# Stick-breaking attention: the second scores of a step issued earlier in TensorE's queue, and one row copy moved up in ScalarE's

## The chip, the cores and the metric

The kernel runs on one core of a Trainium2 chip. The metric is the device time of one execution in microseconds (us); lower is better. Engines: TensorE (PE in the profile, its weight loads PEld), VectorE (DVE), ScalarE (ACT), GpSimd (POOL), and SyncE (SP), which issues most of the transfers.

## The reference, cut to what matters

Two decoder layers over 1024 tokens of width 1024, in float32. Layer 0 mixes tokens with a gated MLP, layer 1 with stick-breaking attention; after each mixer comes a squared-ReLU MLP of hidden width 4096. The change lies in the attention alone, which has 16 heads of 64 and query blocks of 128 rows:

```python
z = einsum('bthd,bshd->bhts', qb, kb) * scale
log_keep = where(causal, log_sigmoid(-z), 0.0)
survive  = cumsum(log_keep, axis=-1, reverse=True) - log_keep
a        = where(causal, exp(log_sigmoid(z) + survive), 0.0)
out      = einsum('bhts,bshd->bthd', a, vb)
```

So each weight is sigmoid(z) times the product of (1 - sigmoid(z)) over the later keys.

## The kernel before, in words

The attention runs as a loop over 8 pairs of heads (`att_step(i)`, i = 0 to 7). A head has 8 tiles, one for each block of 128 query rows; tile t has (t + 1) x 128 keys. Tiles are worked off in pairs (2m, 2m + 1). A step n of `att_step` finishes one pair, m = `ORDER[n % 4]`, with ORDER = 0, 1, 3, 2; there are 8 steps per i, four for each of the two heads. Four steps in a row (m = 0, 1, 3, 2) are called a round here, and its steps a, b, c and d. There are 16 rounds.

What happens to a tile, and the letters used from here on (the figure behind S, B, Q, R and M is the tile of its head, the figure behind K, A and V is the group g of two key blocks):

- S: `scores` on TensorE writes z into one of two PSUM buffers, that of the tile's parity (L1238), then adds the causal mask (L1240). It waits for the R of the tile before the last one, which frees the buffer.
- B: `break_tile` on ScalarE, the sigmoid of z, from PSUM to SBUF (L1654).
- Q: `keep_tile` on ScalarE, the sigmoid of -z, in place in PSUM (L1660).
- R: `sticks` on VectorE, the running product along the row (L2142). It waits for Q.
- M: `stick_mult` on GpSimd, B's result times the shifted product (L910).
- K: `to_keys` on TensorE, up to four transposes of 128x128 of the pair's weights, of key blocks 2g and 2g + 1 (L1255), into one of two PSUM banks in turn. It waits for the copy A that read that bank before.
- A: `keys_in` on ScalarE, which copies a K's bank to SBUF (L1668).
- V: `values` on TensorE, the products of A's result with v (L1268). They run one step later than the K and A of their group.

A pair m has groups g = 0 to m. In step n the scores are those of the pair two steps ahead, `scores(i, 2n + 4)` and `scores(i, 2n + 5)`: tiles 6 and 7 in step a, 4 and 5 in step b, 0 and 1 in step c (of the next head), 2 and 3 in step d. Each engine works its instructions off in the order in which they were written; between engines there are semaphores only. After every other step ScalarE and VectorE also evict a finished output (`out_hi`, L1675, and `out_lo`, L2149). In the first `att_step`, ScalarE and GpSimd also split two blocks of the next stage's weights (L1333, L804), behind steps n = 2 and n = 4.

The order of a round on TensorE before, with V of the step ahead:

```
step a: S6  K0 V0           S7  V1 V2
step b: S4  K0 V0 K1        S5
step c: S0  K0 V0 K1 K2     S1  K3 V1
step d: S2  K0 V0 K1 K2     S3  V1 V2 V3
```

and on ScalarE:

```
step a: B6 A0 Q6    B7 Q7
step b: B4 A0 Q4 A1 B5 Q5        out_hi
step c: B0 A0 Q0 A1 B1 Q1 A2 A3
step d: B2 A0 Q2 A1 B3 Q3 A2     out_hi
```

Of the kernel before, what the change touches and what calls it, by code (L numbers as in the profile page):

```python
# [175 lines left out]
def wait(eng, sem, value):  # L176

    if isinstance(value, int) and value <= 0:
        return
    eng.wait_ge(sem, value)  # L180
# [17 lines left out]
def iterate(eng, n, emit):  # L198

    emit(0)  # L200
    if n > 2:
        with eng.Fori(1, n - 1) as i:
            emit(i)
    if n > 1:
        emit(n - 1)
# [16 lines left out]
QP = NT // 2  # L222
# [4 lines left out]
def pair(n):  # L227

    return ORDER[n % QP]


def groups_before(n):

    return (n // QP) * GH + sum(m + 1 for m in ORDER[:n % QP])


def tile_of(k):

    m, e = pair(k // 2), k % 2
    return (k // NT) % 2, m, e, 2 * m + e  # L240


def build(nc, x, g_mix_pre, g_mix_post, g_ffn_pre, g_ffn_post, w_in, v_g, v_b, w_s, b_s, w_aout,
          w_qkv, w_bout, w1, w2, out):
    ctx = ExitStack()
    with ctx:
# [682 lines left out]
        def _(pe):  # L929
# [297 lines left out]
            def scores(i, k):  # L1227

                hb, _, zb, tb = tile_of(k)
                if tb == 0:  # L1230
                    pe.wait_ge(qk_in[hb], (i + k // (2 * NT)) * (6 * 16) + 6 * 16)
                wait(pe, stick_done, i * (2 * NT) + (k - 1))
                s = (tb + 1) * P
                for c0 in range(0, s, HALF):

                    c1 = c0 + max(2 * P, min(HALF, s - c0))
                    for n in range(2):
                        mm = pe.matmul(z_ps[zb][:, c0:c1], q_st[hb][:, tb * P:(tb + 1) * P], k_st[hb][n][:, c0:c1],  # L1238
                                       start=(n == 0), stop=(n == 1 and c1 < s))
                mm = pe.matmul(z_ps[zb][:, s - P:s], ident_bf[:], mask_bf[:], start=False, stop=True)  # L1240
                mm.then_inc(z_done, 1)

            def to_keys(i, n, g):

                m, gi = pair(n), groups_before(n) + g
                if g == 0:
                    pe.wait_ge(a_done, i * (2 * NT) + (2 * n + 2))
                wait(pe, aT_in, i * (2 * GH) + (gi - 1))
                for p in (2 * g, 2 * g + 1):
                    for e in range(2):  # L1250
                        if p == 0 and e == 0:
                            continue
                        col = (1 - e) * P + (2 * m + 1 - p) * P
                        at_col = (p % 2) * 2 * P + e * P
                        mm = pe.transpose(psum[:, 4 + gi % 2, at_col:at_col + P], brk[m][e][:, col:col + P], ident[:])  # L1255
                mm.then_inc(aT_psum, 1)

            def values(i, n, g):

                m, hb = pair(n), (n // QP) % 2  # L1260
                if g == 0 and n % QP == 0:
                    pe.wait_ge(vh_in[hb], i * 16 + 16)
                if g == 0 and n % 2 == 0:

                    wait(pe, o_split, i * 4 + (n // 2 - 1))
                pe.wait_ge(aT_in, i * (2 * GH) + (groups_before(n) + g + 1))
                for p in (2 * g, 2 * g + 1):
                    mm = pe.matmul(psum[:, 6 + m // 2, (m % 2) * 2 * P:(m % 2 + 1) * 2 * P],  # L1268
                                   v_st[hb][:, 2 * m + 1 - p, :], aT[n % 2][:, p * 2 * P:(p + 1) * 2 * P],
                                   start=(p == 0), stop=(p == 2 * m + 1))  # L1270
                mm.then_inc(av_done, 1)

            def att_step(i):
                first, last = isinstance(i, int) and i == 0, isinstance(i, int) and i == HEADS // 2 - 1
                if first:
                    for k in range(4):
                        scores(0, k)
                    pe.wait_ge(rows_set, 2)
                for n in range(2 * QP):
                    more = not (last and n >= 2 * QP - 2)  # L1280
                    if more:
                        scores(i, 2 * n + 4)

                    here = pair(n) + 1
                    before = 0 if first and n == 0 else pair(n - 1) + 1

                    def prior(g):
                        if g < before:
                            if n:
                                values(i, n - 1, g)  # L1290
                            else:
                                values(i - 1, 2 * QP - 1, g)

                    to_keys(i, n, 0)
                    prior(0)
                    for g in range(1, min(3, here)):
                        to_keys(i, n, g)
                    if more:
                        scores(i, 2 * n + 5)
                    if here > 3:  # L1300
                        to_keys(i, n, 3)
                    for g in range(1, 4):
                        prior(g)
            iterate(pe, HEADS // 2, att_step)
            for g in range(pair(2 * QP - 1) + 1):
                values(HEADS // 2 - 1, 2 * QP - 1, g)
# [4 lines left out]
            for u in range(D // UC):  # L1311
                ready(U_O + u)
                last = u == D // UC - 1
                for t in range(NT):

                    before = 3 if not last or t < 2 else 1
# [12 lines left out]
        def _(act):  # L1329
            def hi(n, b, w=wt, raw=stage):  # L1330

                act.wait_ge(unit_landed, n * 16 + 16)
                act.activation(w[b][0][:], raw[:], ACT.Copy).then_inc(unit_hi, 1)  # L1333
# [315 lines left out]
            def break_tile(i, k):  # L1649
                _, m, e, tb = tile_of(k)  # L1650
                act.wait_ge(z_done, i * (2 * NT) + (k + 1))

                wait(act, aT_psum, i * (2 * GH) + groups_before(k // 2 - QP + 1))
                act.activation(brk[m][e][:, (1 - e) * P:(2 * m + 2) * P], z_ps[e][:, 0:(tb + 1) * P],  # L1654
                               ACT.Sigmoid, scale=SCALE).then_inc(brk_done, 1)

            def keep_tile(i, k):
                _, m, e, tb = tile_of(k)
                act.wait_ge(brk_done, i * (2 * NT) + (k + 1))
                act.activation(z_ps[e][:, 0:(tb + 1) * P], z_ps[e][:, 0:(tb + 1) * P],  # L1660
                               ACT.Sigmoid, scale=-SCALE).then_inc(keep_done, 1)

            def keys_in(i, n, g):
                gi, c0 = groups_before(n) + g, P if g == 0 else 0
                act.wait_ge(aT_psum, i * (2 * GH) + (gi + 1))

                wait(act, av_done, i * (2 * GH) + groups_before(n - 1))
                act.activation(aT[n % 2][:, g * HALF + c0:(g + 1) * HALF], psum[:, 4 + gi % 2, c0:HALF],  # L1668
                               ACT.Copy).then_inc(aT_in, 1)

            def out_hi(i, r):
                h2, g = r // 2, r % 2
                half = slice(h2 * HD, (h2 + 1) * HD)
                act.wait_ge(av_done, i * (2 * GH) + groups_before(2 * r + 2))
                act.activation(hT[0][half, bass.ds(i, 1), g * HALF:(g + 1) * HALF], psum[half, 6 + g:7 + g, :],  # L1675
                               ACT.Copy).then_inc(o_hi, 1)

            def att_step(i):
                first, last = isinstance(i, int) and i == 0, isinstance(i, int) and i == HEADS // 2 - 1
                if first:  # L1680
                    for k in range(4):
                        break_tile(0, k)
                        keep_tile(0, k)
                    act.wait_ge(qk_out[1], 32 * (2 * D // UC) // 2)
                for n in range(2 * QP):

                    out = None if n % 2 == 0 or (first and n == 1) else (i, n // 2 - 1) if n > 1 else (i - 1, 3)
                    more = not (last and n >= 2 * QP - 2)
                    for g in range(4):
                        if more and g < 2:  # L1690
                            (break_tile if g == 0 else keep_tile)(i, 2 * n + 4)
                        if more and g == 2:
                            break_tile(i, 2 * n + 5)
                            keep_tile(i, 2 * n + 5)
                        if g <= pair(n):
                            keys_in(i, n, g)
                    if out:
                        out_hi(*out)
                    if first and n in (2, 4):
                        hi(U_O + n // 2 - 1, n // 2 - 1)  # L1700
            iterate(act, HEADS // 2, att_step)
            out_hi(HEADS // 2 - 1, 3)

# [508 lines left out]
```

## Time and profile before

| | |
|---|---|
| median of 3 runs | 2658.44 us (2658.29 to 2661.26) |
| time of the profiled execution | 2658.29 us |
| its span, first to last instruction | 2656.6 us |
| TensorE busy | 2526.7 us, 95% |
| VectorE / GpSimd / ScalarE busy | 56% / 42% / 39% |
| attention loop, first to last instruction of it | about 1554 to 1892 us |

The span is the time between the first and the last instruction on the core. Busy shares are means over stages that have different limits, so for a change in the attention the rows of that stretch count.

### The profile page before, as it was taken

What the parts mean: (1) busy time and instruction counts of PE and PEld (TensorE: products, weight loads), DVE (VectorE), ACT (ScalarE), POOL (GpSimd) and SP (SyncE); (2) the same over time, 40 slices, a digit from 0 to 9 for tenths busy, and PEclk for the clock granted to TensorE, in tenths of its full rate; (3) what the DMA queues carried; (4) which work ended last, traced back from release to release, by engine and by line L of the source; (5) the groups of instructions that cost most, each with busy time, mean ns of one, the idle gap of its engine ahead of it and who ended that gap; (6) DMA issues with size and microseconds to landing.
All of it is one profiled execution on the core that took longest, in us unless ns stands there. A gap on an engine that the chain in (4) does not pass through costs nothing.

```text
span 2656.6 us, 35493 instructions
## 1 busy us (share of the span) xinstructions
PE 2526.7 (95%) x13100; PEld 2146.0 (81%) x13100; DVE 1484.8 (56%) x1959; ACT 1032.4 (39%) x1507; POOL 1108.1 (42%) x716
## 2 busy tenths in 40 slices
PE   7998999998999999998999988999997999999997
PEld 7997888876888887887998867777886888888886
DVE  3214555658655588776511135656348655588775
ACT  5222221225444433334311147877334444433332
POOL 2221211225555546556222225544235555556554
PEclk9999999999999999999999999999999999999998
DMA  5222112122444464354323635444122544554443
GB/s 167 95 82 109 49 63 80 63 103 88 167 153 153 153 232 162 124 178 147 119 96 142 189 111 127 112 101 103 61 75 92 171 152 151 197 213 158 139 168 114
DMA packets 180417, 342.56 MB, mean 129 GB/s; under 512 B 12224, under 2 KB 95168, under 8 KB 178240
## 3 DMA queue, kind: packets, MB, share of 16 engines
q1 hardware_dynamic: 173632, 311.47, 36.0%
q10 hardware_dynamic: 6656, 29.36, 2.7%
q8 instruction: 82, 1.34, 0.2%
q14 instruction: 47, 0.39, 0.0%
HBM read 235.95 MB, written 104.86 MB: 128 GB/s over the span
## 4 chain that ended last, share of the span: by engine, by line
PE 79%; DVE 8%; issue 4%; ACT 4%; DMA 3%; POOL 2%; SPq 0%; ACTq 0%; DVEq 0%; POOLq 0%
PE psum L1133 22%; PE psum L1179 17%; PE psum L950 13%; PE psum L937 12%; PE psum L961 5%; PE psum L1268 3%; DVE stick L2142 2%; PE psum L1238 2%; PE psum L1255 2%; PE psum L1054 1%; DMA a_raw<-a_forms 1%; ACT psum L1660 1%; POOL rw_lo L891 1%; DVE ra_lo L2022 1%; DVE acc L1741 1%
## 5 line engine op out<-in xcount | busy, mean ns | idle before, releaser
L1179 PE MATMUL psum<-rw_hi,ra_hi 128*128 128x512 f32 x896 | 353.0, 394 | 19.2 <-DVE acc L2040 15.0
L1179 PE MATMUL psum<-rw_lo,ra_hi 128*128 128x512 f32 x896 | 351.4, 392 | 0.0
L1179 PE MATMUL psum<-rw_hi,ra_lo 128*128 128x512 f32 x896 | 351.4, 392 | 0.0
L804 POOL TENSOR_TENSOR w_lo<-stage,w_hi 128x1024 fp32r<-128x1024 f32 x56 | 134.2, 2417 | 504.0 <-ACT w_hi L1333 504.0
L891 POOL TENSOR_TENSOR rw_lo<-blk,rw_hi 128x512 fp32r<-128x512 f32 x152 | 231.7, 1554 | 184.6 <-ACT rw_hi L1483 184.6
L2142 DVE TENSOR_TENSOR_SCAN stick<-psum,brk 128x128 f32<-128x128 f32 (+7 forms) x128 | 173.3, 1355 | 134.1 <-ACT psum L1660 132.7
L2022 DVE TENSOR_TENSOR ra_lo<-a_raw,ra_hi 128x512 fp32r<-128x512 f32 x224 | 226.7, 1020 | 25.0 <-ACT ra_hi L1472 24.9
L1472 ACT ACTIVATE ra_hi<-a_raw 128x2048 fp32r<-128x2048 f32 x56 | 107.4, 1917 | 341.0 <-PE psum L1179 220.1
L910 POOL TENSOR_TENSOR brk<-brk,stick 128x128 f32<-128x128 f32 (+7 forms) x128 | 153.1, 1206 | 196.8 <-DVE stick L2142 196.2
L950 PE MATMUL psum<-w_hi,hT_hi 128*128 128x256 f32 x768 | 219.3, 286 | 1.4 <-DVE hT_lo L2149 1.4
L950 PE MATMUL psum<-w_lo,hT_hi 128*128 128x256 f32 x768 | 218.1, 284 | 0.0
L950 PE MATMUL psum<-w_hi,hT_lo 128*128 128x256 f32 x768 | 218.1, 284 | 0.0
L1179 PEld LDWEIGHTS psum<-rw_hi,ra_hi 128*128 128x128 f32 x896 | 170.0, 190 | 58.5 <-issue 16.1
L1179 PEld LDWEIGHTS psum<-rw_hi,ra_lo 128*128 128x128 f32 x896 | 169.8, 189 | 36.1
L1179 PEld LDWEIGHTS psum<-rw_lo,ra_hi 128*128 128x128 f32 x896 | 170.0, 190 | 35.0
L2040 DVE TENSOR_TENSOR acc<-psum,acc 128x512 f32<-128x512 f32 x192 | 131.4, 686 | 116.4 <-PE psum L1179 116.4
L1268 PE MATMUL psum<-aT,v_st 128*128 128x256 f32 x640 | 159.2, 384 | 0.0
L950 PEld LDWEIGHTS psum<-w_hi,hT_hi 128*128 128x128 f32 x768 | 148.5, 193 | 1.9 <-DVE hT_lo L2149 1.8
L950 PEld LDWEIGHTS psum<-w_lo,hT_hi 128*128 128x128 f32 x768 | 148.4, 193 | 0.0
L950 PEld LDWEIGHTS psum<-w_hi,hT_lo 128*128 128x128 f32 x768 | 148.2, 193 | 0.0
L1238 PE MATMUL psum<-k_st,q_st 128*128 128x512 f32 (+2 forms) x384 | 110.7, 398 | 30.4 <-DVE stick L2142 29.0
L804 POOL TENSOR_TENSOR wq_lo<-stage_q,wq_hi 128x1024 fp32r<-128x1024 f32 x24 | 57.0, 2395 | 191.6 <-ACT wq_hi L1333 191.6
(229 smaller groups left out, 6394.2 us busy)
## 6 DMA issues: line engine op xcount, KB each, us to landing
a_raw<-a_forms SPq DMA_DIRECT2D x56, 1024.0 KB, 5.6
a_forms<-a_out SPq DMA_DIRECT2D x64, 512.0 KB, 3.1
blk<-mlp_w_in SPq DMA_DIRECT2D x28, 1024.0 KB, 5.3
a_forms<-a_out SPq DMA_DIRECT2D x32, 768.0 KB, 3.3
stage<-a_w_in_in SPq DMA_DIRECT2D x16, 1024.0 KB, 5.4
stage<-mlp_w_in SPq DMA_DIRECT2D x16, 1024.0 KB, 6.0
raw<-mlp_w_in SPq DMA_DIRECT2D x32, 512.0 KB, 5.0
x_res<-xt SPq DMA_DIRECT2D x24, 512.0 KB, 4.9
```

The costliest lines, as they stand in the source:

```text
L804: pool.tensor_tensor(w[b][1][:, c], raw[:, c], w[b][0][:, c].bitcast(F32), ALU.subtract).then_inc(unit_ready, 1)
L891: ins = pool.tensor_tensor(w[1][:, k, :], src[:, k, :], w[0][:, k, :].bitcast(F32), ALU.subtract)
L910: pool.tensor_tensor(brk[m][e][:, c0:c1], brk[m][e][:, c0:c1], stick[m][e][:, c0 + 1:c1 + 1], ALU.mult).then_inc(a_done, 1)
L937: mm = pe.matmul(psum[:, bank, :], w[ub][sw][:, k * UC + f * P:k * UC + (f + 1) * P], h[sh][:, k, half * HALF:(half + 1) * HALF], start=(n ...
L950: mm = pe.matmul(psum[:, bank, c0:c0 + UC], h[sh][:, k, t * P:(t + 1) * P], w[ub][sw][:, k * UC:(k + 1) * UC], start=(n == 0), stop=(n == ...
L961: mm = pe.matmul(psum[:, 4 + j % 4, :], a_buf[ab][sa][:, r, t * P:(t + 1) * P], wt[ub][sw][:, r * D + n2 * HALF:r * D + (n2 + 1) * HALF], ...
L1133: mm = pe.matmul(psum[:, bank, :], W[p][sw][:, k, :], H[layer][p][sh][:, k, :], start=(p in (1, 2, 5) and n == 0), stop=(p in (4, 2, 3) an ...
L1179: mm = pe.matmul(psum[:, down_bank(n, tp), :], ring_a[n % 3][sa][:, k, tp * P:(tp + 1) * P], ring_w[n % 3][sw][:, k, :], start=(p in (1, 2 ...
L1238: mm = pe.matmul(z_ps[zb][:, c0:c1], q_st[hb][:, tb * P:(tb + 1) * P], k_st[hb][n][:, c0:c1], start=(n == 0), stop=(n == 1 and c1 < s))
L1268: mm = pe.matmul(psum[:, 6 + m // 2, (m % 2) * 2 * P:(m % 2 + 1) * 2 * P], v_st[hb][:, 2 * m + 1 - p, :], aT[n % 2][:, p * 2 * P:(p + 1) * ...
L2022: ins = dve.tensor_tensor(ring_a[n % 3][1][:, k, :], a_raw[n % 2][:, k, :], ring_a[n % 3][0][:, k, :].bitcast(F32), ALU.subtract)
L2142: dve.tensor_tensor_scan(row, keep, unused, 1.0, ALU.mult, ALU.bypass).then_inc(stick_done, 1)
```

## The change

On TensorE, `scores(i, 2n + 5)` is issued right behind K0 and V0 in every step, where before it came behind K1 and K2; and K and V of the same group now alternate (K1 V1 K2 V2 and so on), where before all K came ahead of V1. On ScalarE, the copy of group 2 is issued between the two sigmoids of tile 2n + 5, where before it came behind both. Orders on VectorE, GpSimd and SyncE are unchanged, and so is every instruction's own work.

```diff
--- before.py
+++ after.py
@@ -1283,24 +1283,16 @@
 
                     here = pair(n) + 1
                     before = 0 if first and n == 0 else pair(n - 1) + 1
-
-                    def prior(g):
+                    for g in range(max(here, before)):
+                        if g < here:
+                            to_keys(i, n, g)
                         if g < before:
                             if n:
                                 values(i, n - 1, g)
                             else:
                                 values(i - 1, 2 * QP - 1, g)
-
-                    to_keys(i, n, 0)
-                    prior(0)
-                    for g in range(1, min(3, here)):
-                        to_keys(i, n, g)
-                    if more:
-                        scores(i, 2 * n + 5)
-                    if here > 3:
-                        to_keys(i, n, 3)
-                    for g in range(1, 4):
-                        prior(g)
+                        if more and g == 0:
+                            scores(i, 2 * n + 5)
             iterate(pe, HEADS // 2, att_step)
@@ -1685,13 +1677,9 @@
                 for n in range(2 * QP):
 
                     out = None if n % 2 == 0 or (first and n == 1) else (i, n // 2 - 1) if n > 1 else (i - 1, 3)
-                    more = not (last and n >= 2 * QP - 2)
                     for g in range(4):
-                        if more and g < 2:
-                            (break_tile if g == 0 else keep_tile)(i, 2 * n + 4)
-                        if more and g == 2:
-                            break_tile(i, 2 * n + 5)
-                            keep_tile(i, 2 * n + 5)
+                        if not (last and n >= 2 * QP - 2):
+                            (break_tile if g % 2 == 0 else keep_tile)(i, 2 * n + 4 + g // 2)
                         if g <= pair(n):
                             keys_in(i, n, g)
```

Written out, the order of a round after the change, on TensorE:

```
step a: S6  K0 V0 S7 V1 V2                (as before)
step b: S4  K0 V0 S5 K1
step c: S0  K0 V0 S1 K1 V1 K2 K3
step d: S2  K0 V0 S3 K1 V1 K2 V2 V3
```

and on ScalarE:

```
step a: B6 A0 Q6    B7    Q7              (as before)
step b: B4 A0 Q4 A1 B5    Q5     out_hi   (as before)
step c: B0 A0 Q0 A1 B1 A2 Q1 A3
step d: B2 A0 Q2 A1 B3 A2 Q3     out_hi
```

## Rows read from the trace of the kernel before

**Rows 1.** The page: the span, and each engine's busy time, share and count.
```profile
span 2656.6 us, 35493 instructions
PE 2526.7 (95%) x13100; PEld 2146.0 (81%) x13100; DVE 1484.8 (56%) x1959; ACT 1032.4 (39%) x1507; POOL 1108.1 (42%) x716
```

**Rows 2.** Windows: stretch, length, busy of PE, PEld, DVE, ACT, POOL, PE clock, DMA.
```profile
1595.00:1605.00 10.00, 4.61 (x17) 3.86 (x18) 3.67 (x4) 3.01 (x7) 9.41 (x7) 0.66 1.03 233
...
1691.38:1711.22 19.84, 18.41 (x110) 15.20 (x109) 12.15 (x11) 15.77 (x29) 9.60 (x8) 1.00 0.45 106
```

**Rows 3.** Waits from 1610 to 1866 us: total us, times, longest.
```profile
DVE stick L2142 <- ACT psum L1660: 97.9, 78, 2.7
...
PEld psum L1238 <- DVE stick L2142: 24.0, 31, 1.1
```

**Rows 4.** Timeline of one steady round, from its S6 to the next S6: start, length.
```profile
1691.38 1.16 PE L1238 MATMUL psum<-k_st,q_st 128*128 128x512 f32 x4
...
1694.97 4.35 DVE L2142 TENSOR_TENSOR_SCAN stick<-psum,brk 128x896 f32<-128x896 f32 x2 [2.66 <-ACT psum L1660]
...
1698.25 1.03 PE L1268 MATMUL psum<-aT,v_st 128*128 128x256 f32 x4
...
1699.12 0.60 PE L1255 MATMUL psum<-ident,brk 128*128 128x128 f32 x4
...
1699.47 0.94 PE L1238 MATMUL psum<-k_st,q_st 128*128 128x512 f32 x4
1699.75 0.60 ACT L1668 ACTIVATE aT<-psum 128x512 f32<-128x512 f32 x1
...
1700.26 0.23 PE L1240 MATMUL psum<-mask_bf,ident_bf 128*128 128x128 bf16 x1
1700.53 0.81 ACT L1654 ACTIVATE brk<-psum 128x768 f32<-128x768 f32 x1 [0.17 <-PE psum L1240]
...
1701.47 0.50 PE L1238 MATMUL psum<-k_st,q_st 128*128 128x256 f32 x2 [0.98 <-DVE stick L2142]
...
1702.19 1.76 DVE L2142 TENSOR_TENSOR_SCAN stick<-psum,brk 128x768 f32<-128x768 f32 x1 [0.78 <-ACT psum L1660]
1702.21 1.03 PE L1268 MATMUL psum<-aT,v_st 128*128 128x256 f32 x4
...
1703.08 1.10 PE L1255 MATMUL psum<-ident,brk 128*128 128x128 f32 x8
...
1704.01 0.50 PE L1238 MATMUL psum<-k_st,q_st 128*128 128x256 f32 x2
...
1704.41 0.61 PE L1255 MATMUL psum<-ident,brk 128*128 128x128 f32 x4
...
1704.86 1.03 PE L1268 MATMUL psum<-aT,v_st 128*128 128x256 f32 x4
...
1705.31 1.08 ACT L1668 ACTIVATE aT<-psum 128x512 f32<-128x512 f32 x2
...
1705.54 0.70 PE L1238 MATMUL psum<-k_st,q_st 128*128 128x384 f32 x2
...
1707.35 1.04 PE L1255 MATMUL psum<-ident,brk 128*128 128x128 f32 x8
...
1708.14 0.72 PE L1238 MATMUL psum<-k_st,q_st 128*128 128x512 f32 x2
...
1708.70 2.47 PEld L1268 LDWEIGHTS psum<-aT,v_st 128*128 128x128 f32 x12
...
1711.22 1.16 PE L1238 MATMUL psum<-k_st,q_st 128*128 128x512 f32 x4
```

**Rows 5.** Timeline of the second round (first two rows) and of the last (third).
```profile
1601.32 0.90 PE L1255 MATMUL psum<-ident,brk 128*128 128x128 f32 x3 [2.18 <-POOL brk L910]
1602.01 1.91 PE L1268 MATMUL psum<-aT,v_st 128*128 128x256 f32 x4
...
1881.71 1.54 POOL L910 TENSOR_TENSOR brk<-brk,stick 128x768 f32<-128x768 f32 x1 [1.27 <-DVE stick L2142]
```

## The prediction

> **What bounds the kernel now.** I read the page first. TensorE is busy for 95% of the span and the next engine for 56% [rows 1], so time is lost wherever TensorE waits, and won only where a wait of it goes away. The change touches only the attention, so I next read the windows there. One steady round takes 19.84 us, with TensorE busy for 18.41 [rows 2]: at most 1.43 us of a round is idle, and with 16 rounds no reordering that leaves the instructions alone can win over 23 us. Then the waits: of TensorE's in 256 us of steady rounds, nearly all are one kind, scores waiting for a scan (24.0 us, 31 times, two or three in a round, the longest 1.1) [rows 3]. Last the timeline of one round [rows 4], where the reader should follow which scores wait, and what TensorE does while a scan is still running. Three places matter:
>
> - S4 in step b waits a little for R6. The change is nowhere ahead of that in the round.
> - S5 comes at 1699.47. Its buffer is freed by R7, the second of two scans that end at 1694.97 + 4.35 = 1699.32. TensorE doesn't wait: V0 (1698.25) and K1 (1699.12) fill the time [rows 4].
> - S0 comes at 1701.47 after 0.98 of waiting for R4. S1 comes at 1704.01. Its buffer is freed by R5, at 1702.19 + 1.76 = 1703.95. Again TensorE hardly waits, because V0 (1702.21) and the eight transposes of K1 and K2 (from 1703.08) lie in that time [rows 4].
>
> So the transposes that the change moves behind S5 and S1 are what TensorE now does while the scans run.
>
> **The change part by part.** Nothing is added or removed: no matmul, copy, wait or DMA. SP's loads of q, k and v hang on counts of scores and values that shift with them. I carry one round through in its new order, from the same S6 (1691.38), with durations and distances from [rows 4]. Distances between starts on TensorE: V to S 0.68 (1704.86 to 1705.54), V to K 0.87 (1702.21 to 1703.08), K of four to V 0.45 (1704.41 to 1704.86), two K of four to the next 0.79 (1707.35 to 1708.14), short S with its mask to K 0.40 (1704.01 to 1704.41). A scan's end to the S that waits for it: 0.06 (1703.95 to 1704.01).
>
> *Step a* keeps its order: 0.
>
> *Step b, S5 ahead of K1.* After V0 TensorE is free at 1698.25 + 0.68 = 1698.93, but S5 has to wait for R7: 1699.32 + 0.06 = 1699.38. So S5 gains only 0.09 and 0.45 us of TensorE goes idle. K1 now follows S5: 0.79 to the mask (1699.47 to 1700.26) and about 0.07 more, so 1700.24, done 0.60 later at 1700.84. This is the step that costs, because ScalarE's order still has A1 ahead of B5. A1 can't start before K1 is done: 1700.87 (0.03 after it, as 1699.72 to 1699.75 now), where it was 1699.75. B5's scores are there at about 1700.4, but B5 is queued behind A1. Two copies in a row take 1.08 where one takes 0.60, so the next instruction starts some 0.50 after the first: B5 at 1701.37 instead of 1700.53, **0.84 later**. Behind B5 on ScalarE stand Q5 and the output copy; R5 waits for Q5, and so R5 ends 0.84 later, at 1704.79. S0 is not touched: it waits for R4 until 1701.47 as now, and K1 is out of the way by then.
>
> *Step c, S1 ahead of K1 and K2.* After V0 TensorE is free at 1702.21 + 0.68 = 1702.89, and S1 has to wait for R5: 1704.79 + 0.06 = 1704.85. That is an empty stretch of **1.96 us**, where before it held K1 and K2. Behind S1 comes all that was ahead of it: K1 (+0.40), V1 (+0.45), K2 (+0.87), K2 and K3 (+0.79), and S2 at 1704.85 + 2.51 = 1707.36, where it was 1705.54: **1.82 late**. K3 needs the A1 that frees its bank. K1 ends at 1705.85, A1 by 1706.5, and K3 is due at about 1707.0, so nothing is added there.
>
> *Step d.* S2 needs R0, which follows R5 and a short eviction and is over by about 1706.0: no wait. S3 is due 0.40 to 0.61 + 0.33 + 0.68 after S2, at about 1709.0. Its buffer is freed by R1. On ScalarE, Q1 now stands behind A2, which waits for K2 (done at about 1707.2): A2 costs Q1 some 0.5, Q1 is done near 1707.9 and R1 (0.7 long) near 1708.65. That leaves 0.3 of cover. If it is gone, the late S3 costs up to the 0.6 us of an A in a round. From S2 to the next S6 TensorE does the same work as before in 1711.22 - 1705.54 = 5.68 us: no change. Q3 behind A2 delays R3, which has until the next S7, 2 us behind S6: hidden by that.
>
> So the next S6 comes about 1.8 us late and everything starts again: nothing in step a gives it back, since S4's wait for R6 is counted from S6 itself. Rounds 3 to 15 are such rounds: 13 x 1.82 = 23.7 us.
>
> *The first two rounds* have GpSimd's weight splits, and TensorE waits for GpSimd (2.18 us, at 1601.32) [rows 5]. A delay of ScalarE in step c moves the split behind it, and the multiplications behind that, so the delay is passed on but hardly adds up. Bounds: 0 (all hidden in that wait) and 2 x 1.82. I take the middle, 1.8. *The last round* has S5 but neither S1 nor S3, and its step d starts on M5, at 1881.71 + 1.54 [rows 5], which comes 0.84 later: 0.8.
>
> The sum is 23.7 + 1.8 + 0.8 = 26.3. The profiled execution took 2658.29 us, which is within 0.2 us of the median, so the forecast is 2658.3 + 26.3 = **2684.6 us**, 1.0% slower.
>
> The clock. At 1595 to 1605 us TensorE stood still for 4 us and then 2 us, and the granted clock of these 10 us was 0.66; in the steady round, whose longest gap is 0.98, it was 1.00 [rows 2, 4, 5]. The new gap of 1.96 lies between them. I take 1.00, because the new round is still busy for 18.4 of 21.7 us.
>
> **The rivals.**
>
> *The clock falls behind the new gap.* V0 at 1602.01 took 1.91 us, behind the two waits, and takes 1.03 in steady rounds [rows 4, 5]. If the clock falls in each round for the 2.51 us from S1 to S2, they take 2.51 x (1.91 / 1.03 - 1) = 2.1 us more, 13 x 2.1 = 28: 2712 us. For it speaks the clock of 0.66, against it that the round stays 85% busy. The Trainium skill ("TensorE: Matmul & The Clock Gate", section "HAM oscillation — how this bites in real kernels") says that a loop which makes TensorE wait in each round can put it back to its lower level each time; by that rule 2712 would be the time. The steady round here has gaps of up to 1 us and shows no fall, so I give it 8%.
>
> *Smaller loss.* If B5 doesn't wait for A1 as I read it (say S5 and K1 are nearer than I put them), S1 comes at 1704.01 as now. Then only the transposes' cover is lost: 0.79 to 1.1 us in a round, 13 x 1 = 13 and little at the ends: about 2672 us. Against it stands the written order of ScalarE. 9%.
>
> *Nothing changes.* The instructions are the same, and if the idle time now in front of S0 and S4 (0.98 and less) took up the moved transposes, the sum would be about 0: 2658 us. Against it: K1 and K2 of step c can't move ahead of S0. 6%.
>
> *Faster.* Scans wait for ScalarE's Q for 97.9 us in 256 [rows 3], about 7.6 in a round. If S5 and S1 start early enough to bring B5, Q5 and R5 forward, S0 and S4 might stop waiting, and the most to win is the 1.43 idle us of a round: 13 x 1.43 = 19 us, 2640 us. It decides at S1: R5 has to end before V0 is issued, at 1702.89, and it ends at 1703.95 even now, so it would have to gain over 1.06. The S5 that starts it can gain 0.09 only, since R7 frees its buffer. 6%.
>
> *The forecast's own case:* 71%.
>
> **How the numbers follow.** The forecast's own range: the sum with nothing from the first rounds and 1.6 in a round gives 2658.3 + 20.8 + 0.8 = 2680; with 3.6 from the first rounds, and S3's cover gone (up to 0.6 in a round, 7.8), 2694. For 8 in 10 I go down to 2670, so that the smaller loss is in, and up to 2698; outside lie the clock, no change and faster, 20% together. Within 0.2% (5.3 us) is about what a measurement of this kernel can't tell from no change: faster 0.06, same 0.06, slower 0.88.
>
> **What would show it.** In the profile after: the round at 21.6 to 21.7 us instead of 19.84; TensorE's work of a round unchanged at 18.4; S1 behind a wait of about 2 us for the scan, and S5 behind one of about 0.4; S0's wait shrunk to about 0.8; ScalarE's B5 right behind A1, and VectorE's wait ahead of R5 longer by 0.84. The granted clock stays 1.00. The prediction is wrong if S1 doesn't wait, if the clock falls, or if S3 waits as well.

## The result and the profile after

The kernel after takes 2691.31 us (median of 4 runs, 2689.78 to 2693.9), the kernel before 2658.36: 1.0122 times as long, 95% interval 1.0105 to 1.014. The forecast was 2684.6 us with 2670 to 2698 around it. So the sign and most of the size were right; of the 33 us lost, 26.3 were forecast.

The page of the kernel after gives the span and TensorE's busy time, to be set against [rows 1]:

```profile
span 2692.1 us, 35493 instructions
PE 2541.5 (94%) x13100; PEld 2150.4 (80%) x13100; DVE 1483.2 (55%) x1959; ACT 1028.1 (38%) x1507; POOL 1110.5 (41%) x716
```

The instructions are the same in number. The waits of the same 256 us as in [rows 3]:

```profile
DVE stick L2130 <- ACT psum L1652: 117.7, 71, 5.2
ACT aT L1660 <- PE psum L1255: 49.9, 58, 2.1
PEld psum L1238 <- DVE stick L2130: 47.3, 46, 2.2
```

Two more rows of that view after, and the same of the kernel before:

```profile
PE psum L1238 <- DVE stick L2130: 30.0, 40, 1.8
...
PE psum L1238 <- DVE stick L2142: 16.8, 26, 1.0
ACT aT L1668 <- PE psum L1255: 6.5, 19, 0.4
```

(the first is after, the other two before). The weight loads of the scores wait for a scan for 47.3 us instead of 24.0, their matmuls for 30.0 instead of 16.8, and ScalarE now waits for the transposes (49.9 us instead of 6.5), which used to be early. The timeline of one round, steps b and c (start, length; the lines of ScalarE and VectorE in `kernel.py` have moved up by 8 and 12), to be set against [rows 4]:

```profile
1687.30 1.03 PE L1268 MATMUL psum<-aT,v_st 128*128 128x256 f32 x4
...
1688.52 0.98 PE L1238 MATMUL psum<-k_st,q_st 128*128 128x512 f32 x4 [0.19 <-DVE stick L2130]
...
1689.40 0.61 PE L1255 MATMUL psum<-ident,brk 128*128 128x128 f32 x4
...
1690.05 0.60 ACT L1660 ACTIVATE aT<-psum 128x512 f32<-128x512 f32 x1 [1.20 <-PE psum L1255]
...
1690.54 0.81 ACT L1646 ACTIVATE brk<-psum 128x768 f32<-128x768 f32 x1
...
1692.20 1.76 DVE L2130 TENSOR_TENSOR_SCAN stick<-psum,brk 128x768 f32<-128x768 f32 x1 [1.83 <-ACT psum L1652]
...
1694.02 0.51 PE L1238 MATMUL psum<-k_st,q_st 128*128 128x256 f32 x2 [1.81 <-DVE stick L2130]
...
1694.87 1.68 PE L1268 MATMUL psum<-aT,v_st 128*128 128x256 f32 x4
...
1696.35 1.91 PE L1255 MATMUL psum<-ident,brk 128*128 128x128 f32 x8
...
1697.91 0.87 PE L1238 MATMUL psum<-k_st,q_st 128*128 128x384 f32 x2
```

Read it downward: S5 right at the scan's end, K1 behind it at 1689.40, A1 only at 1690.05 after 1.20 us of idle ScalarE, B5 behind A1, R5 with 1.83 us of wait in front (0.78 in [rows 4]), and S1 at 1694.02 after 1.81 us in which TensorE did nothing. That is the chain of the forecast. But the lines under S1 are longer than the forecast had them: V1 takes 1.68 us, not 1.03, and K2 with K3 1.91, not 1.04. From S1 to S2 it is 3.89 us, not 2.51. The windows of two rounds that follow each other (S6 to S6), and of S1 to S2 in each, say why:

```profile
1659.05:1680.61 21.56, 18.77 (x110) 14.96 (x109) 12.15 (x11) 15.52 (x29) 9.61 (x8) 1.00 0.41 98
1680.61:1703.71 23.10, 20.41 (x110) 16.25 (x109) 12.00 (x11) 15.33 (x29) 9.56 (x8) 0.93 0.38 91
...
1672.53:1675.04 2.51, 2.51 (x19) 2.31 (x20) 1.10 (x2) 1.02 (x3) 1.92 (x2) 1.00 1.03 219
1694.02:1697.91 3.89, 3.89 (x19) 3.43 (x20) 0.84 (x2) 1.34 (x3) 1.92 (x2) 0.64 1.03 215
```

Behind the length stand the busy times of the five engines, and then the granted clock. In the first round S1 to S2 runs at 1.00 and takes 2.51 us, as worked out; in the second it runs at 0.64 and takes 3.89. That 0.64 is a mean of the clock's two levels, 1.00 (2.4 GHz) and 0.50 (1.2 GHz), as a shorter window within it shows:

```profile
1695.30:1698.30 3.00, 3.00 (x12) 2.61 (x12) 0.00 (x0) 1.50 (x5) 0.72 (x2) 0.50 0.89 180
```

Of the 13 steady rounds nine take 21.47 to 21.58 us and four take 23.07 to 23.16. Steady rounds come in two kinds that alternate (why wasn't traced): before, 19.85 and 19.68 us; after, 21.56 and 21.48 where the clock stays up. All four falls lie in rounds of the shorter kind, so one fall costs 23.12 - 21.48 = 1.64 us. Without falls the 13 rounds would take 21.52 on average (six of either kind, and the last, which took 21.54), 1.77 more than before.

The 35.5 us between the two profiled executions (2693.77 against 2658.29) thus lie so: 13 rounds x 1.77 = 23.0; four falls of the clock 29.5 - 23.0 = 6.5 (S6 of the third round to S6 of the last: 1615.98 to 1902.34 after, 1612.32 to 1869.16 before); the first two rounds 3.9 (from the S7 of the first, at 1562.95 after and 1563.18 before, to the S6 of the third); the last round 0.9 (S6 to the next stage's first matmul: 23.98 against 23.03); 1.4 behind the attention, and 0.2 less ahead of it.

### The profile page after: what moved, and what is told of

It is laid out like the page before. It is cut to its first block, busy times and chain, and to the rows that moved or that the text cites. A ratio compares the mean times of both kernels' runs of the same rounds, so it can differ in the third digit from the quotient of the medians.

```text
span 2692.1 us, 35493 instructions
## 1 busy us (share of the span) xinstructions
PE 2541.5 (94%) x13100; PEld 2150.4 (80%) x13100; DVE 1483.2 (55%) x1959; ACT 1028.1 (38%) x1507; POOL 1110.5 (41%) x716
## 3 DMA queue, kind: packets, MB, share of 16 engines
q1 hardware_dynamic: 173632, 311.47, 35.5%
## 4 chain that ended last, share of the span: by engine, by line
PE 77%; DVE 9%; ACT 4%; issue 4%; DMA 3%; POOL 2%; SPq 0%; ACTq 0%; DVEq 0%; POOLq 0%
PE psum L1133 22%; PE psum L1179 16%; PE psum L950 13%; PE psum L937 12%; PE psum L961 5%; PE psum L1268 3%; DVE stick L2130 2%; PE psum L1255 2%; PE psum L1238 2%; ACT psum L1652 1%; PE psum L1054 1%; DMA a_raw<-a_forms 1%; DVE ra_lo L2010 1%; ACT brk L1646 1%; POOL rw_lo L891 1%
## 5 line engine op out<-in xcount | busy, mean ns | idle before, releaser
L2010 DVE TENSOR_TENSOR ra_lo<-a_raw,ra_hi 128x512 fp32r<-128x512 f32 x224 | 228.5, 1029 | 21.8 <-ACT ra_hi L1464 21.6
L1268 PE MATMUL psum<-aT,v_st 128*128 128x256 f32 x640 | 165.2, 390 | 0.0
```

The source lines that it names most:

```text
L2010: ins = dve.tensor_tensor(ring_a[n % 3][1][:, k, :], a_raw[n % 2][:, k, :], ring_a[n % 3][0][:, k, :].bitcast(F32), ALU.subtract)
```

## The experiments

A round's length is the mean of the 13 steady rounds, S6 of the third to S6 of the last, in the profiled execution. The kernel before was run beside each group, and its medians there were 2661.6 to 2662.4 us, so ratios are compared and not times. The last column has the round that the theory of each expectation gives; the two lines with "again" were run side by side.

| run | ratio to before (95% interval) | round, us | expected round |
|---|---|---|---|
| kernel before | | 19.76 | |
| kernel after | 1.0122 (1.0105 to 1.014) | 22.03 (21.52 without falls) | 21.6 |
| S5 alone | 1.0043 (1.0028 to 1.0057) | 20.66 | 20.7 |
| S1 and S3 alone | 1.0037 (1.0023 to 1.0051) | 20.63 | 20.8 |
| ScalarE alone | 0.9996 (0.9986 to 1.0006) | 19.76 | 19.8 |
| after, B5 ahead of A1 | 1.0055 (1.0038 to 1.0072) | 20.95 | 20.7 |
| after, gap filled | 1.0114 (1.0098 to 1.0129) | 21.52 | 21.5 |
| after, again | 1.0108 (1.0092 to 1.0123) | 21.78 | 21.5 and 23.1 |
| after, gap filled, again | 1.0107 (1.0092 to 1.0122) | 21.53 | 21.5 |
| V0 ahead of S0 | 0.9988 (0.9979 to 0.9997) | 19.62 | 19.4 |
| the same, R0 earlier | 0.9996 (0.9987 to 1.0005) | 19.62 | 19.1 |
| the same, A2 earlier | 0.998 (0.9971 to 0.9989) | 19.42 | 19.15 |
| the same, V0 ahead of K0 in step d | 0.9964 (0.9951 to 0.9978) | 19.30 | 19.1 to 19.2 |

**S5 ahead of K1, alone.**

```diff
                     prior(0)
+                    if more and n % QP == 1:
+                        scores(i, 2 * n + 5)
                     for g in range(1, min(3, here)):
                         to_keys(i, n, g)
-                    if more:
+                    if more and n % QP != 1:
                         scores(i, 2 * n + 5)
```

> The kernel before with S5 ahead of K1 in step b alone; steps c and d and ScalarE's order as before. Theory: K1 comes later, ScalarE's A1 with it, and B5, queued behind A1, with that. B5, R5 and S1 are 0.84 us later in each round, K1 and K2 still cover the wait ahead of S1, and S2 follows at the old distance. Rounds of 20.7 us instead of 19.8, 13 x 0.84 = 11 and about 1.5 at the ends: 2671 us. No gap of TensorE above 1 us, so a granted clock of 1.00. Rival: the whole loss is the lost cover in step c, and this edit costs nothing: 2658 us.

Rounds became 0.90 us longer. Its timeline shows the same queue on ScalarE as after: K1, A1 behind 1.09 us of idle time, B5, and then the late R5.

```profile
1706.09 0.60 PE L1255 MATMUL psum<-ident,brk 128*128 128x128 f32 x4
1706.73 0.60 ACT L1670 ACTIVATE aT<-psum 128x512 f32<-128x512 f32 x1 [1.09 <-PE psum L1255]
1707.22 0.81 ACT L1656 ACTIVATE brk<-psum 128x768 f32<-128x768 f32 x1
...
1708.89 1.76 DVE L2144 TENSOR_TENSOR_SCAN stick<-psum,brk 128x768 f32<-128x768 f32 x1 [1.64 <-ACT psum L1662]
```

The rival, that this part is free, falls.

**S1 and S3 ahead of K1 and K2, alone.**

New lines alone; they replace the whole old order of K, V and the second scores:

```diff
+                    if n % QP == 1:
+                        to_keys(i, n, 0)
+                        prior(0)
+                        to_keys(i, n, 1)
+                        if more:
+                            scores(i, 2 * n + 5)
+                    else:
+                        for g in range(4):
+                            if g < here:
+                                to_keys(i, n, g)
+                            prior(g)
+                            if more and g == 0:
+                                scores(i, 2 * n + 5)
```

> The kernel before with TensorE's new order in steps a, c and d alone; step b and ScalarE's order as before. Theory: S1 waits for R5 at its old time with nothing in front of it, an empty stretch of 1.1 us, and K1 and K2 come behind it: S2 0.98 us later, rounds of 20.8 us, 13 x 0.98 = 12.7 and about 1 in the first rounds: 2672 us, clock 1.00. Rival 1: all the loss comes over B5, and this costs nothing: 2658 us. Rival 2: a gap of 1.1 us is already enough for the clock to fall in some rounds: each fall adds 1.5 us.

Rounds became 0.87 us longer, with S1 behind a new wait:

```profile
1687.57 1.03 PE L1268 MATMUL psum<-aT,v_st 128*128 128x256 f32 x4
1689.47 0.50 PE L1238 MATMUL psum<-k_st,q_st 128*128 128x256 f32 x2 [0.87 <-DVE stick L2145]
...
1689.88 0.61 PE L1255 MATMUL psum<-ident,brk 128*128 128x128 f32 x4
```

From S1 to S2 it is 2.51 us instead of 1.53, and from S2 to the next S6 5.57 instead of 5.68. The edit also lets K and V alternate, and no run has the one without the other; but the 0.87 is about what the eight transposes take that used to stand ahead of S1 (0.93, from 1703.08 to 1704.01 in [rows 4]), so little is left for the alternation. With the first experiment this adds up: 0.90 + 0.87 = 1.77, and the whole change costs 1.77 in a round without a fall. No steady round was longer than 20.72 us: behind these gaps of 0.77 and 0.87 us the clock didn't fall.

**ScalarE's order alone.**

Without the line that sets `more`, which goes as well:

```diff
-                        if more and g < 2:
-                            (break_tile if g == 0 else keep_tile)(i, 2 * n + 4)
-                        if more and g == 2:
-                            break_tile(i, 2 * n + 5)
-                            keep_tile(i, 2 * n + 5)
+                        if not (last and n >= 2 * QP - 2):
+                            (break_tile if g % 2 == 0 else keep_tile)(i, 2 * n + 4 + g // 2)
```

> The kernel before with ScalarE's new order alone (group 2's copy ahead of Q1 and Q3). Theory: Q1 and R1 come some 0.5 us later, but S3 is due over 1.5 us after R1's end in the order before: 2658 us, rounds of 19.8 us. Rival: each delayed scan reaches TensorE, 0.5 us a round: 2665 us.

The 13 rounds took 256.84 us, to the hundredth what they take before. Q1 is late, as the timeline shows (B1, A2, Q1), and nobody was waiting for it:

```profile
1704.10 0.38 ACT L1654 ACTIVATE brk<-psum 128x256 f32<-128x256 f32 x1 [0.30 <-PE psum L1240]
1704.38 0.59 ACT L1668 ACTIVATE aT<-psum 128x512 f32<-128x512 f32 x1
1704.86 0.39 ACT L1660 ACTIVATE psum<-psum 128x256 f32<-128x256 f32 x1
```

In the kernel after, no S3 of a steady round waits either.

**After, with B5 ahead of A1 on ScalarE.** The order of step b there is B4 A0 Q4 B5 A1 Q5.

```diff
-                        if not (last and n >= 2 * QP - 2):
+                        more = not (last and n >= 2 * QP - 2)
+                        if more and not (n % QP == 1 and g == 2):
                             (break_tile if g % 2 == 0 else keep_tile)(i, 2 * n + 4 + g // 2)
+                        if more and n % QP == 1 and g == 1:
+                            break_tile(i, 2 * n + 5)
```

> The kernel after with B5 ahead of A1 on ScalarE in step b, all else as after. Theory: the 0.84 us a round are given back (11 us), the gap ahead of S1 shrinks from 1.8 to about 1.1 us and with that the clock no longer falls behind it (another 6 us): about 2673 us, as with S1 and S3 moved alone. Rival 1: the clock falls all the same in some rounds: 2679 us. Rival 2: A1, now behind B5, delays K3's bank or the values and costs up to 0.6 us a round of what is won: 2680 us.

The round is 0.57 us shorter than after without falls, not 0.84. The second rival had named A1, but by way of K3's bank or the values; the timeline shows another way:

```profile
1708.02 0.81 ACT L1646 ACTIVATE brk<-psum 128x768 f32<-128x768 f32 x1 [0.65 <-PE psum L1240]
1708.73 0.59 ACT L1660 ACTIVATE aT<-psum 128x512 f32<-128x512 f32 x1
...
1709.20 0.82 ACT L1652 ACTIVATE psum<-psum 128x768 f32<-128x768 f32 x1
...
1711.87 0.50 PE L1238 MATMUL psum<-k_st,q_st 128*128 128x256 f32 x2 [1.06 <-DVE stick L2133]
```

A1 stands between B5 and Q5, so Q5 comes at 1709.20 where B5 ended at 1708.83: 0.37 us of the old delay are still there. The gap ahead of S1 is 1.06 us here and 1.24 in rounds of the other kind, and all 13 rounds take 20.91 to 20.99: no fall of the clock.

**After, with the gap filled.** K1's four transposes run three more times ahead of S1, with nothing waiting for them (`extra=True` leaves out the count of the semaphore); they change no result. The place of the call:

```diff
                         if more and g == 0:
+                            if n % QP == 2:
+                                for _ in range(3):
+                                    to_keys(i, n, 1, extra=True)
                             scores(i, 2 * n + 5)
```

> The kernel after with the four transposes of K1 of step c run three times more ahead of S1, into the bank that K1 writes right behind; nothing waits for the extra ones. TensorE thus works for about 1.4 of the 1.8 us that it stood still, and nothing on the path from R5 to S1 changes. Theory: four of the 13 steady rounds of the kernel after took 23.1 us instead of 21.55 because the granted clock fell behind the gap; with the gap filled all rounds take 21.5 to 21.6 us, the clock stays 1.00 there, and the time is 4 to 6 us less: 2686 us. Rival 1: the falls have another cause: rounds of 23.1 us remain, 2691 us. Rival 2: the extra transposes reach beyond R5's end or slow others: longer than 2692 us.

All 13 rounds took 21.48 to 21.56 us, 21.52 on average, which is the length worked out above for the kernel after without falls. The time of the whole kernel did not settle it (1.0114 beside 1.0122, the intervals overlap), so both were run once more on one chip.

> The kernel after, unchanged, beside the next one on the same chip. Theory: rounds of 21.5 us with some of 23.1 us, where the granted clock falls in the 4 us behind S1: 1.0122 of the time before.

> The kernel after with the gap ahead of S1 filled with extra transposes of K1, beside the kernel after on the same chip. Theory: no round of 23.1 us, so 4 to 6 us less than the kernel after in the same job, a ratio to the kernel before about 0.002 lower. Rival: the same time as the kernel after, with the slow rounds there by chance in the one profiled execution only.

The kernel after had two rounds of 23.13 and 23.12 us this time, both of the shorter kind, and eleven of 21.48 to 21.56; the filled one again none. Its timeline, with the extra transposes in front of S1, and the windows from V0 to S1 and from S1 to S2:

```profile
1693.51 1.47 PE L1255 MATMUL psum<-ident,brk 128*128 128x128 f32 x12
1695.48 0.50 PE L1238 MATMUL psum<-k_st,q_st 128*128 128x256 f32 x2 [0.50 <-DVE stick L2134]
```

```profile
1692.64:1695.48 2.84, 2.34 (x19) 1.95 (x17) 1.81 (x2) 2.16 (x6) 0.71 (x1) 1.00 0.96 235
1695.48:1697.99 2.51, 2.51 (x20) 2.32 (x20) 0.85 (x2) 1.03 (x3) 1.91 (x2) 1.00 1.03 217
```

So in two profiles of the kernel after 6 of 26 steady rounds had a fall, and in two of the filled one 0 of 26. From the third round's S6 to the next stage's first matmul the filled kernel took 303.8 us both times, the kernel after 310.3 and 307.1. Yet the whole time didn't drop (1.0107 beside 1.0108): behind the attention the filled kernel took 770.5 and 771.3 us, the kernel after 765.7 and 767.6. TensorE waits for VectorE's additions in the second MLP's down part for 8.5 and 8.8 us there, against 3.8 in the kernel after's second profile:

```profile
PE psum L1179 <- DVE acc L2032: 8.8, 2, 5.0
```

```profile
PE psum L1179 <- DVE acc L2028: 3.8, 1, 3.8
```

(the first is the filled kernel, the second the kernel after, both from the end of the attention on). It needn't come from the extra transposes: the kernel "A2 earlier" below has none, and took 769.5 us behind the attention, with 7.6 us of that wait. The eleven profiles of the other kernels, before and after among them, have 764.4 to 769.5 us there. Why is open. That the fall of the clock lengthens a round by 1.64 us is measured; that filling the gap is worth anything over the kernel is not.

**Values the other way: V0 ahead of S0, V1 ahead of K1, in step c.** Not shown: the usual call for S0 is skipped in this step.

```diff
+                    if n % QP == 2:
+                        prior(0)
+                        if more:
+                            scores(i, 2 * n + 4)
+                        to_keys(i, n, 0)
+                        prior(1)
+                        to_keys(i, n, 1)
+                        to_keys(i, n, 2)
+                        if more:
+                            scores(i, 2 * n + 5)
+                        to_keys(i, n, 3)
+                        continue
```

> The kernel before with step c's values moved the other way: V0 ahead of S0, where TensorE waits 0.9 to 1.0 us for R4, and V1 ahead of K1 and K2, so that behind S1 there is K3 alone. ScalarE's order as before. Theory: S1 stays at R5's end, and of the 0.68 us taken out behind S1 S2 gets only 0.35, because R0 ends 0.35 us ahead of S2's old time: 13 x 0.35 = 4.5, about 2654 us. Rival 1: the path from S1 to S2 isn't TensorE's work, and nothing changes: 2658 us. Rival 2: V0 delays S0 beyond R4's end and the chain over K0, K1, K2 with it: slower, up to 0.5 us a round, 2665 us.

And with VectorE's eviction of step b's output moved behind R0:

> The kernel before with V0 ahead of S0 and V1 ahead of K1 in step c, and on VectorE R0 ahead of the output's eviction of step b, which ran between R5 and R0. Theory: R0 ends 0.7 us earlier, so S2 gets all of the 0.68 us: 13 x 0.68 = 9, about 2649 us. Rival: S2 didn't wait for R0, and this gives the same as without VectorE's edit.

Both have rounds of 19.62 us, 0.14 shorter than before, and S2 comes early as meant. What it won is lost one line later (the timeline of the second of the two, with S1, S2, the copies A2 and A3, and K0 of step d):

```profile
1705.37 0.50 PE L1238 MATMUL psum<-k_st,q_st 128*128 128x256 f32 x2
...
1706.14 0.60 PE L1238 MATMUL psum<-k_st,q_st 128*128 128x384 f32 x2
...
1706.68 1.08 ACT L1680 ACTIVATE aT<-psum 128x512 f32<-128x512 f32 x2
...
1707.32 0.55 PE L1255 MATMUL psum<-ident,brk 128*128 128x128 f32 x3 [0.51 <-ACT aT L1680]
```

S2 is 0.77 us behind S1 (1.53 before). Then K0 of step d waits 0.51 us for its PSUM bank, which the copy A2 (1706.68) empties. In the first of the two, R0 did hold S2, as expected: S2 is 1.18 us behind S1 (0.90 in rounds of the other kind), and K0 follows at 1708.26, again at A2's end:

```profile
1706.30 0.50 PE L1238 MATMUL psum<-k_st,q_st 128*128 128x256 f32 x2
...
1707.48 0.62 PE L1238 MATMUL psum<-k_st,q_st 128*128 128x384 f32 x2 [0.17 <-DVE stick L2154]
...
1707.61 1.08 ACT L1680 ACTIVATE aT<-psum 128x512 f32<-128x512 f32 x2
...
1708.26 0.55 PE L1255 MATMUL psum<-ident,brk 128*128 128x128 f32 x3
```

So K0 is 1.96 and 1.95 us behind S1 in the two. The earlier R0 brought S2 forward, but not the round: that is why the expected 0.35 and 0.68 both came out as 0.14.

**A2 of step c ahead of B1.**

```diff
+                        if n % QP == 2 and g == 2:
+                            keys_in(i, n, 2)
                         if more and g == 2:
                             break_tile(i, 2 * n + 5)
                             keep_tile(i, 2 * n + 5)
-                        if g <= pair(n):
+                        if g <= pair(n) and not (n % QP == 2 and g == 2):
                             keys_in(i, n, g)
```

> As with V0, V1 and R0 moved, and ScalarE's copy A2 of step c ahead of B1 and Q1. In the trace of the two runs with V0 ahead of S0, S2 came 0.6 us earlier, and then K0 of step d stood 0.51 us for the copy A2 (its PSUM bank), which is queued behind B1 and Q1. Theory: A2's transposes are done 0.4 us ahead of B1's scores, so it fits in front, K0 no longer waits, and the round falls from 19.62 to about 19.15 us: 13 x 0.6 = 8 us below the kernel before, 2650 us beside 2658. Rival: another wait takes its place (S3 for R1, since B1 comes later, or S6's chain): no change from 19.6 us.

It gave 0.20 us of the expected 0.47. The wait for the copy went, and the transposes now waited for GpSimd's products, 0.33 us in a round. By its place in the round that is K0 of step d for M5. The waits of TensorE's transposes from 1615 to 1860 us:

```profile
PE psum L1255 <- POOL brk L910: 3.9, 12, 0.3
```

**V0 ahead of K0 in step d as well.** Step d is then S2 V0 K0 K1 K2 S3 V1 V2 V3.

> As the kernel with the bank copy moved up, and in step d V0 ahead of K0. In the trace of that kernel K0 of step d stood up to 0.5 us for M5, GpSimd's product of tile 5, and V0 was ready all along. Theory: V0 fills this wait, K0 follows 0.87 us behind it with M5 done, and the wait goes, less about 0.3 us that K2 then has to wait for its bank's copy A0: rounds of 19.1 to 19.2 us instead of 19.42, 13 x 0.25 = 3 us less: a ratio to the kernel before of 0.997. Rival: K2's or S3's wait takes all of it: 19.4 us, 0.998.

Rounds of 19.30 us, 0.46 less than before, and a ratio of 0.9964 (0.9951 to 0.9978). It is the fastest of all, 0.4% below the kernel before. The wait for M5 is gone, but only half of the expected 0.2 to 0.3 us came of it (0.12), so the round misses the expected 19.1 to 19.2.

## Why the prediction was right, and where it was too low

- *The transposes cover the scans.* Right. S5 came only 0.10 us earlier in the kind of round that the forecast used, because R7 frees its buffer, and S1 nothing. The two parts cost 0.90 and 0.87 us alone and add up to the whole.
- *A1 holds B5 back by 0.84.* Right: with that edit alone R5 ends 0.86 and 0.94 us later in the two kinds of rounds, and the round is 0.90 longer.
- *S2 1.82 late in each round.* Right in size, with a small luck in it: S1 came 0.85 to 0.94 late, S1 to S2 took the 2.51 as worked out, and step d, which the forecast left at 5.68, took 5.57. A round without a fall is 1.77 longer.
- *TensorE's waits.* The 24.0 us of [rows 3] are those of the weight loads; the matmuls' own were 16.8 us. The sum does not use either. S1's wait was to be 1.96 and is 1.63 or 1.81 in the profile, and TensorE's busy time 18.77 and not 18.4: the forecast let V0 end where the next instruction could start, 0.68 behind its start, while the profile counts its whole 1.03. The 0.35 between them goes from the one to the other.
- *Step d free, and ScalarE's edit with it.* Right: 0.00 with that edit alone, and S3 waits in no steady round after.
- *The first two rounds 1.8, at most 3.6.* Too low: 3.9 in the first profile and 3.2 in the second. GpSimd's splits came 2.8 us later, counted from the first S6, and the work behind its wait, which ran at a low clock before too, now held S1 and V1 as well. The size is uncertain: all this is against one profile of the kernel before (51.4 us for the two rounds), and the kernel with ScalarE's order alone took 53.4 for them, with the same steady rounds.
- *The last round 0.8.* 0.9.
- *The clock.* This is the step that failed. "I take 1.00, because the new round is still busy for 18.4 of 21.7 us" was wrong in four of 13 rounds of the first profile and two of the second. Each such round is 1.64 us longer, not the 2.1 of the rival, and only some rounds are hit, so the term is 6.5 and 3.3 us, where the rival had 28. The truth lay between the two cases; the forecast had no case for a fall in some rounds, and its range took the term in without having foreseen it. The Trainium skill ("TensorE: Matmul & The Clock Gate", section "HAM oscillation — how this bites in real kernels") tells of a matmul loop that falls back to the lower level behind its wait in every turn, with waits longer than those here. The trace agrees with it for 6 of 26 rounds, and not for the other 20.
- *Faster was held out by R5's end at 1703.95.* Right for this order. The idle time of a round could be won by other moves, but all of those tried here together won 0.46 of the 1.43 us.

## What to carry to other kernels

Before moving work out from in front of an instruction, ask what releases that instruction: if it is a later event than the end of the work in front, the work was free there and is on the path anywhere else. On an engine that takes its queue in order, look at the copy of the moved work on the next engine too; here half the loss came over a 0.6 us copy that stood in front of the sigmoid that mattered. When a wait is taken away, name the next one before counting the gain: the values moved ahead of S0 here met first a PSUM bank and then GpSimd's product, and only with both out of the way did 0.4% come of it.

## What the runs showed of the hardware that was not expected

The granted clock fell behind gaps of TensorE that differ by very little. In the steady rounds of the first profile of the kernel after, six waits ahead of S1 were 1.80 or 1.81 us long, and behind four of them the granted clock was 0.57 to 0.68 over the 4 us from S1 on; seven were 1.62 to 1.74 long, none followed by a fall. In the second profile it was two of six (1.80 to 1.82) and none of seven (1.62 to 1.75). Earlier gaps don't fit a limit: in the first round a wait of 2.50 wasn't followed by a fall (S1 to S2 took 2.51 us there), one of 1.98 in the second profile was (3.92 us), and one of 1.96 with S1 and S3 moved alone wasn't. So a gap's length alone doesn't tell, and what else decides is open. Twelve transposes in the gap, 1.47 us long, were enough to keep the clock at 1.00 in 26 of 26 steady rounds.
